# One pair of convolution inputs moved ahead of the latent projections, norm columns by whole transposes, and dummy matmuls under the first loads, in a three-layer transformer kernel

## The reference, cut to what matters

```python
for l in range(2):
    x = x + 0.5 * swiglu(rms_norm(x, ffn1_norm[l]), ffn1_wi[l], ffn1_wo[l])
    u = rms_norm(x, mix_norm[l])
    c = split_cols(u @ w_in[l] + b_in[l])      # sb_q/k/v, ml_q/k/v/o/i/f, cq, ckv, kr, gates
    y_sb  = stick_breaking_attention(c['sb_q'], c['sb_k'], c['sb_v'])
    y_ml  = mlstm(silu(causal_conv4(c['ml_q'], c['ml_k'])), c['ml_v'], ...)   # 4 heads of 128
    y_mla = mla(rms_norm(cq) @ wq_up, rms_norm(ckv) @ wkv_up, ...)            # softmax, 4 heads
    g = sigmoid(c['gates'])                    # 3 x 1024
    x = x + (g0*(y_sb @ w_up_sb) + g1*(y_ml @ w_up_ml) + g2*(y_mla @ w_up_mla)) @ w_out[l]
    x = x + 0.5 * swiglu(rms_norm(x, ffn2_norm[l]), ffn2_wi[l], ffn2_wo[l])
```

## Time and profile before

| | |
|---|---|
| runs | 2365.41 us median of 3 (2364.04 to 2365.55) |
| the profiled execution | 2363.47 us, span 2361.7 us |
| PE busy | 2340.2 us, 99% of the span |
| PEld, DVE, ACT, POOL busy | 1909.7, 1124.1, 982.9, 1288.7 us |
| DMA | 212.88 MB, mean 90 GB/s |

### The profile page before, as it was taken

The page is one execution under the profiler, slowest core; times in us unless marked ns, Lnnn a source line. Parts: engine busy times, 40 slices in busy tenths (PEclk is TensorE's granted clock), DMA queues, the critical chain, the costliest instruction groups (busy, mean ns, idle before and its releaser), DMA issues.

```text
span 2361.7 us, 29592 instructions
## 1 busy us (share of the span) xinstructions
PE 2340.2 (99%) x11084; PEld 1909.7 (81%) x11084; DVE 1124.1 (48%) x1820; ACT 982.9 (42%) x1561; POOL 1288.7 (55%) x1589
## 2 busy tenths in 40 slices
PE   8999999999999999999999999999999999999999
PEld 8777788888888888777788888888887777888887
DVE  5765375422324432478626733333325785265330
ACT  4566543222223233676534432332336764343321
POOL 5654266655556655456245755555554553466554
PEclk9999999999999999999999999999999999999999
DMA  5322133333333333222122333333332221233333
GB/s 163 100 73 70 55 92 96 99 98 98 96 94 110 99 98 105 72 64 79 54 90 81 99 99 98 97 91 98 98 104 65 71 72 56 88 92 97 97 98 98
DMA packets 60862, 212.88 MB, mean 90 GB/s; under 512 B 6704, under 2 KB 8112, under 8 KB 60720
## 3 DMA queue, kind: packets, MB, share of 16 engines
q1 hardware_dynamic: 60576, 210.86, 29.6%
q10 hardware_dynamic: 144, 0.14, 0.0%
HBM read 208.87 MB, written 2.10 MB: 89 GB/s over the span
## 4 chain that ended last, share of the span: by engine, by line
PE 98%; ACT 1%; DVE 1%; issue 0%; DMA 0%; POOL 0%; SPq 0%; ACTq 0%
PE banks L749 96%; PE banks L1048 0%; PE banks L878 0%; ACT t L1742 0%; PE banks L928 0%; DMA t<-in_xT 0%; DVE t L1251 0%; PE banks L1105 0%; POOL t L2073 0%; DVE t L1440 0%; ACT t L1871 0%; ACT L2034 0%; DVE t L1596 0%; DVE t L1677 0%; DVE t L1478 0%
## 5 line engine op out<-in xcount | busy, mean ns | idle before, releaser
L749 PE MATMUL banks<-t,t 128*128 128x512 f32 (+8 forms) x10796 | 2315.8, 385 | 17.6 <-ACT t L1762 6.3
L749 PEld LDWEIGHTS banks<-t,t 128*128 128x128 f32 (+3 forms) x10796 | 1878.0, 187 | 433.5 <-issue 49.7
L2073 POOL TENSOR_TENSOR t<-t,t 128x256 fp32r<-128x256 f32 x1544 | 1234.4, 830 | 1036.6 <-ACT t L1742 1027.8
L1742 ACT ACTIVATE t<-t 128x1024 fp32r<-128x1024 f32 x385 | 408.2, 1060 | 1087.0 <-issue 584.9
L1251 DVE TENSOR_TENSOR t<-banks,t 128x512 f32<-128x512 f32 x121 | 83.1, 688 | 187.0 <-PE banks L749 186.6
L1421 DVE TENSOR_TENSOR t<-banks,t 128x512 f32<-128x512 f32 x44 | 30.4, 691 | 184.1 <-PE banks L749 184.0
L1389 DVE SCALAR_TENSOR_TENSOR t<-banks,t 128x512 f32<-128x512 f32 x32 | 22.1, 691 | 155.4 <-PE banks L749 155.4
L1134 DVE SCALAR_TENSOR_TENSOR t<-t,t,t 128x512 fp32r<-128x512 f32 x64 | 51.9, 815 | 58.2 <-ACT t L1762 58.1
L1366 DVE TENSOR_TENSOR t<-t,t 128x512 fp32r<-128x512 f32 x68 | 70.1, 1031 | 2.3
L1762 ACT ACTIVATE t<-t,t 128x512 fp32r<-128x512 f32 x64 | 45.5, 715 | 55.6 <-DVE t L1389 48.8
L1395 DVE TENSOR_TENSOR t<-banks,t 128x512 f32<-128x512 f32 x24 | 16.6, 691 | 106.0 <-PE banks L749 106.0
(11 more groups left out here) (190 smaller groups left out, 1224.3 us busy)
## 6 DMA issues: line engine op xcount, KB each, us to landing
t<-in_w SPq DMA_DIRECT2D x386, 512.0 KB, 3.5
t<-in_xT SPq DMA_DIRECT2D x8, 256.0 KB, 6.0
out<-t SPq DMA_DIRECT2D x8, 256.0 KB, 4.6
t<-in_vbias SPq DMA_DIRECT2D x2, 384.0 KB, 3.9
t<-in_c SPq DMA_DIRECT2D x1, 576.0 KB, 9.1
t<-in_w SPq DMA_DIRECT2D x2, 256.0 KB, 4.1
t<-in_pos SPq DMA_DIRECT2D x2, 256.0 KB, 3.7
t<-in_dmask SPq DMA_DIRECT2D x4, 128.0 KB, 4.3
```

The costliest lines, as they stand in the source:

```text
L749: return pe.matmul(o, l, r, start=start, stop=stop, skip_group_check=True)
L1742: a.activation(whl[u % 2][:, 0:1024], wraw[u % 3][:, :], ACT.Copy).then_inc(*w_high.next(u))
L2073: p.tensor_tensor(hl[:, 1024:2048][:, c], wraw[u % 3][:, c], as_f32(hl[:, c]), ALU.subtract).then_inc(*w_low.next((u, q)))
```

## The change

Three edits. (1) In each mixer the last mlq/mlk pair is projected ahead of kup, qup and vup instead of behind them; `plan()` follows. (2) `columns` makes four whole 128 x 128 transposes into the columns 384 to 511 of the banks 0 to 3 (or into one bank), and the copy takes the first column of each; the strided set in the first block is made from a copy that DVE rearranges first, and is asked for later. (3) DVE clears `rstdB` at the start, and TensorE multiplies these zeros in three float32 matmuls of 512, 512 and 256 columns before its first real work.

```diff
@@ plan()
-        for t in range(1, 3):
+        for t in range(1, 4):
             both("mlq", "mlk", t)
         ... (kup, qup, vup)
         while len(out) % 8:
             out.append(("pad", None, 0, None, None))
-        both("mlq", "mlk", 3)
@@ build_program
+        def turned(b, o):
+            return banks_t[:, 0:4, o:o + 128] if o else B[b].rearrange("p (c n) -> p c n", c=4)
@@ tensor_program
+            def warm():
+                need.wait_ge(*v_norm.at(("warm",)))
+                for n in (512, 512, 256):
+                    mm(B[7][:, 0:n], rstdB[:, 0:128], rstdB[:, 0:n])
@@ columns (tensor)
-                    ins = mm(B[b][:, o + c:o + c + 1], view(src, c), C["ident"][:, 0:1])
+                    ins = pe.transpose(turned(b, o)[:, c, :], view(src, c), C["ident"])
@@ vector_program
+            def warm():
+                v.memset(rstdB, 0.0).then_inc(*v_norm.next(("warm",)))
@@ columns (vector)
-                v.tensor_copy(dst, B[b][:, o:o + 4]).then_inc(*v_norm.next(("cols", name)))
+                v.tensor_copy(dst, turned(b, o)[:, :, 0]).then_inc(*v_norm.next(("cols", name)))
+                if name == ("rc", 1):
+                    v.tensor_copy(sqt.rearrange("p (r n) -> p r n", r=4),
+                                  rstdB.rearrange("p (n r) -> p r n", r=4)).then_inc(*v_norm.next(("rstd_strided",)))
@@ the steps
         put("load_cols")
+        put("warm")
         put("load_front")
...
             put("cols", ("rc", 1), 0, 384, rstdB, natural, rcol_t[:, 0:4], (v_norm, ("rstd", 0)))
-            put("cols", ("rc", 2), 1, 384, rstdB, strided, rcol_t[:, 4:8], (v_norm, ("rstd", 0)))
+            yield "t", (v_norm, ("rstd_strided",))
+            put("cols", ("rc", 2), 0, 384, sqt, natural, rcol_t[:, 4:8], (v_norm, ("rstd_strided",)))
@@ mixer
-            for t_ in range(1, 3):
+            for t_ in range(1, 4):
                 ml_proj(t_)
             sch.until(("low", l), *[("sb", l, t_) for t_ in range(2)])
...
-            ml_proj(3)
```

More of the change, by code:

```diff
@@ L342 @@
     FIRST = {"norm": "av", "norm_halves": "av", "norm_squares": "av", "head_in": "av", "low_halves": "pav", "conv": "av", "halves1": "av", "half2": "av", "stats": "tav", "stats_beside": "tav",
-             "whalf": "avp", "whalf_rest": "ap", "sb_split": "av", "low_rs": "av"}
+             "warm": "vt", "whalf": "avp", "whalf_rest": "ap", "sb_split": "av", "low_rs": "av"}
     def put(self, *step):
@@ L1107, in ml_turn @@
                 bank[ba] = [(v_attn, ("ml_open", l, h))]
-            return {"mm": dense, "wide": wide, "small_turn": small_turn, "stats": stats, "stats_beside": stats_beside, "cols": columns, "head_sum": head_sum, "dil_scores": dil_scores, "dil_turn": dil_turn, "dil_values": dil_values,
+            return {"warm": warm, "mm": dense, "wide": wide, "small_turn": small_turn, "stats": stats, "stats_beside": stats_beside, "cols": columns, "head_sum": head_sum, "dil_scores": dil_scores, "dil_turn": dil_turn, "dil_values": dil_values,
                   "swa_scores": swa_scores, "swa_turn": swa_turn, "swa_values": swa_values, "sb_scores": sb_scores,
@@ L1703, in merge2 @@
                 split(MH[m][0], MH[m][1], T[tl[0]], ("mixed", l, m))
-            return {"whalf": half_weights, "norm": norm, "norm_halves": norm_halves, "norm_squares": norm_squares, "stats": stats, "cols": columns, "turns1": turns1, "turns2": turns2,
+            return {"warm": warm, "whalf": half_weights, "norm": norm, "norm_halves": norm_halves, "norm_squares": norm_squares, "stats": stats, "cols": columns, "turns1": turns1, "turns2": turns2,
                     "rope_angles": rope_angles, "values1": values1, "proj": proj, "head_in": head_in, "key_rope": key_rope,
```

## The result

The changed kernel takes 2375.43 us (median of 6 runs, 2374.45 to 2377.95), the kernel before in the same session 2364.74 us (6 runs, 2364.04 to 2365.55). The ratio is 1.0047 with a 95% interval of 1.0037 to 1.0057: slower, by 10.7 us. The forecast was 2372.1 us and +6.7 us.

What follows compares the result with a forecast made beforehand. The prediction took PE's single stream of matmuls as the bound: columns -3.5, start 0, mixers +10.2 made +6.7 us, so a median of 2372.1 us. Its own range was 2369 to 2375, the wide range 2365 to 2376.

Steps and rivals of the forecast that it cites:

- The start, 0: Dummy matmuls at the start: faster first matmuls only reach gates on POOL and DMA sooner, so 0 us.
- Rival 2: Start: the clock pays in full, gaining 2.7 us, the rest as forecast; +4.0, 2369.4 us; chance 0.13.
- Rival 4: Start: the clock falls in the new pauses there, +3 us, 2375 us; chance 0.06.
- The columns, -3.5: All column sets: transposes replacing one-column matmuls save 3.5 us of PE time, between 2.7 and 4.0.
- The term for the strided set: Strided column set in the first block: made natural, it falls from 2.06 to 0.44 us, saving 1.6 us.
- that for the first natural set: Each natural column set: from 0.81 to 0.44 us with four transposes; five such sets save 1.9 us.
- The moved pair, +10.2: Both mixers: projections gone from under the heads' chains add 5.5 us idle each, less 0.4 saved; 10.2 us.
- The wait for head 8's square: Each mixer behind vup: PE, done with the transposes at 11.3, waits 2.4 us for this square on ACT.
- the kup wait: Ahead of the latent projections: PE's wait for kup's bank stays; 0.4 us a mixer saved here and behind transposes.
- Rival 1: Mixers: the new idle time is half covered, 2.5 us a mixer; +1.5, 2366.9 us; chance 0.15.
- Rival 3: Mixers: the pair covers waits ahead of kup and the silus end in time; -8.5, 2356.9 us; chance 0.11.
- Rival 5: Whole kernel: the change hardly does anything, lists re-laid with the same sum; +-1.5 us; chance 0.05.

Runs made afterwards that it cites:

- e_warm: Kernel before with only the dummy matmuls and their memset added: 2364.49 us against 2364.65, ratio 0.9998.
- e_nopair: Changed kernel without the moved pair, so columns edit and dummy matmuls only: 2360.15 us against 2364.73 for the kernel before, ratio 0.9981.
- e_cols: Kernel before with only the columns edit (transposes and DVE's rearranging copy): 2360.48 us against 2364.65, ratio 0.9983.
- e_strided: Kernel before with only the strided set turned whole, the five other sets left as one-column matmuls: 2362.25 us against 2364.73, ratio 0.9988.
- e_pair: Kernel before with only the last mlq and mlk pair moved ahead of the latent projections: 2379.56 us against 2364.65, ratio 1.0062.
- e_fillstart: Kernel before with the dummy matmuls and nine more unread matmuls ahead of the third slice of inputs: 2364.53 us against 2364.52, ratio 1.0000.
- e_repeat: Kernel before with the strided one-column matmuls issued three times over (24 instead of 8): 2369.33 us against 2364.73, ratio 1.0018.
- e_fillmix: Changed kernel with unread matmuls in two pauses of each mixer (ten and eight): 2370.70 us, ratio 1.0028 to the kernel before.
- e_late: Changed kernel with the silus held back until the last four query heads are done: 2374.95 us, ratio 1.0040 to the kernel before.
- e_gate4: Changed kernel with four gate units instead of five allowed ahead of the unfinished heads: 2383.32 us, ratio 1.0079 to the kernel before.

## Why the prediction was right, point by point

**The start, 0.** Right, though not in the one profile that came with the result. There the start is 1.0 us late. Over all profiles it is +1.1 to -0.5 us with the dummy matmuls (eight, mean 0.0) and +0.6 to -0.4 without (five, mean +0.1). The gates are what the prediction said: PE came early and waited for POOL. The third slice started at 13.1 as predicted (12.5 in e_warm, 14.1 in e_nopair); the fifth at 18.9, not 17.6, behind a fall of the clock (17.1 in e_warm). In the other seven profiles with dummy matmuls the clock did not fall at the start. e_nopair had a pause of 1.8 us on record there and stayed at 1.00:

```profile
9.99 2.35 PE L753 MATMUL banks<-t,t 128*128 128x384 f32 x12 [1.84 <-DVE t L1146]
14.13 4.43 PE L753 MATMUL banks<-t,t 128*128 128x384 f32 x24 [1.79 <-POOL t L2088]
```

Rival 2 (the clock pays in full) is out by e_warm. Rival 4 named this fall and the time 2375, and the time came out at that: a coincidence, since e_nopair, with the same start, is 4.6 us faster than the kernel before, and the start was only 1.0 us late in the profile that has the fall.

**The columns, -3.5.** 3.05 us in the profile of e_cols, inside the bounds of 2.7 to 4.0. The term for the strided set was too large (1.6, measured 1.2 in e_strided), that for the first natural set a little small (0.37, measured 0.5), and the other four gave 1.3 of 1.5. The transposes in the changed kernel:

```profile
42.41 0.60 PE L849 MATMUL banks<-t,t 128*128 128x128 f32 x4
42.76 3.19 PE L752 MATMUL banks<-t,t 128*128 128x512 f32 x12
```

The next matmul starts 0.35 us behind the first of them, where 0.44 was taken. So the figure of the Trainium skill (TensorE: Matmul & The Clock Gate, Part 4), which that page gives for bf16, fits the duration of one transpose, but not what each of several costs when they follow each other: e_cols won 3.05 us where the sum of durations leaves 0. What the step did not see is the 1.1 us on top of it in the timed runs. Its source is for the greater part a fall of the clock at the old strided set, which e_cols has in none of its 11 runs and the kernel before in 13 of the 21 beside them; against the 8 others e_cols wins 3.5 us. The fall was seen in three profiles (e_pair, e_fillstart, e_repeat), all with the old sets, and in none of the eight without the strided one; before and e_warm have it and did not fall there. So the profile of the kernel before, which every comparison of profiles rests on, is one of the minority without the fall. The last 0.5 us, 3.5 against 3.05, stays open.

**The moved pair, +10.2.** The chain was right to within 0.3 us at each of its points, and so was the order of the waits. Without the clock the pair costs 5.0 and 5.3 us a mixer, where 5.1 was forecast; by the times, e_fillmix less e_nopair is 2370.70 - 2360.15 = 10.5 us, and 10.8 when each is taken against the kernel before beside it. Two details differ. The wait for head 8's square is 1.4 us in layer 0 (2.0 in layer 1) and not 2.4, as the slow transposes took the rest, and the kup wait was kept in full; of the 0.4 us that were to be saved, 0.3 was, at the transposes (L1048 above). The step that failed is one that is not in the sum: the mixers' own pauses let the clock fall. The prediction looked for that danger only at the start, as rival 4, and not at the 2.2 us wait in the mixers that it had itself worked out. That costs 1.5 + 2.4 = 3.9 us by the profiles and 4.7 by the times (the changed kernel less e_fillmix), where half of the changed kernel's runs had a further fall. With it the forecast would have been 2376 to 2377; the columns, 0.7 us better than forecast, took a little of that back.

The Trainium skill (TensorE: Matmul & The Clock Gate, Part 1, on the oscillation of the clock) describes matmul groups that each start slow because the wait ahead of them dropped the level; this trace agrees, 0.50 behind 2.1 us of idle time, though the waits on that page are longer. It prices that as the slow time x (1 - 1.2/2.4). With 6.8 us in each mixer that page's rule is an estimate of 6.8 us; 3.9 was measured. PE is idle for 1.5 us of the stretch in layer 0 anyway.

**The rivals.** Rival 1 (half covered) is out by the table. Rival 3 (faster) turned on whether the silus end in time; e_late, where they are out of the way, costs as much as the changed kernel, since the waits only change place. Rival 5 is out.

**The range**, 2365 to 2376, held the time near its upper end; the forecast's own range, 2369 to 2375, was missed by 0.4 us. That the wide one held is partly luck: its room upward was for longer waits and a fall at the start, and it was used up by falls in the mixers, which it has no term for. The probabilities leaned the right way.

**What stays open:** why the clock falls behind the pause at the start in one profile of eight and in seven of the eight mixers that have the pause (e_late's second one is the exception, and e_late had a pause of 1.96 us at the start without a fall), and what it is in the old strided set that brings the fall.

## What to carry to other kernels

A pause can be priced twice: by the wait itself, and by the work behind it at half the clock, so for each new wait of some 2 us on TensorE look at what is queued behind it. Work that looks freely movable may be the cover of someone else's chain: take half of it away and then one piece more, and the slack shows as the kink in the cost. One profile is one draw of the clock; where a theory rests on it, compare the same stage over all the profiles at hand.

## What the hardware showed that was not expected

- The granted clock fell to 0.50 behind idle stretches of 2 us (in e_late behind two of 1.3 us with little work between), for 3.4, 6.8 or 10.2 us (the last in both mixers of e_gate4, beginning inside 5.6 us idle, and in layer 0 of e_pair); with fillers in the same pauses it stayed at 1.00. Pauses of 1.3, 1.3 and 2.6 us in layer 1 of e_late brought no fall.
- It fell also where PE was never idle by the page, behind 2.7 us of one-column matmuls (3.4 us long) and, with 24 in place of 8 strided ones, for 6.8 us, beginning between them 4 us behind the first.
- The page's row of the clock, in slices of 59 us, shows none of these falls; the windows do, and the mean granted clock of a run counts them (0.996 against 1.000).
- Table loads stand at 1.28 us each in every timeline here.
